# Feed-forward stage: the last round's four up tiles in a row, and the down products before them taken between the last gate's operations

## The chip, the cores and the metric

The kernel runs on one core of one Trainium2 chip. The metric is the device time of one execution in microseconds, lower is better. The core has TensorE (PE, matrix products), VectorE (DVE), ScalarE (ACT), GpSimd (POOL) and SyncE (SP, which only issues DMAs here). Each engine works through its own program in order and waits on semaphores for the others.

## The reference

One decoder layer is run for a prompt group (1024 tokens) and a sample group (8 times 4 tokens), 1056 tokens in all. The change lies in the last part of the layer, the feed-forward with a short convolution along the tokens:

```python
D_MODEL = 1024; D_FF = 2816; CONV_W = 3
def conv_ffn(h, conv_prev, w_up, conv_w, conv_b, w_down):
    T = h.shape[1]
    u = h @ w_up                                   # 1024 -> 2 * 2816
    up = jnp.concatenate([conv_prev.astype(u.dtype), u], axis=1)
    c = conv_b + sum(conv_w[j] * up[:, j:j + T] for j in range(CONV_W))
    gate, val = jnp.split(c, 2, axis=-1)
    return (jax.nn.silu(gate) * val) @ w_down, up[:, T:]

# in the layer: x = x + f, and after it y = rmsnorm(x, g_final)
```

## The kernel before

Everything is kept transposed: 128 features on the partitions, 1056 tokens along the free side, cut into three pieces of 352. Each fp32 product is made of three matmuls (high times high, high times low, low times high), in `products` (L276 to L281), which gives one semaphore step at its end. Such a product over a group of 128 features and 352 tokens is called a group here.

The stage `ffn_stage` takes the 2816 hidden features in 22 blocks, two blocks to a round, `ROUNDS` = 11, counted 0 to 10. A block has two up tiles, its gate half and its value half, so a round has four up tiles. An up tile is 3 groups of 24 matmuls. Numbered through, the last round has up tiles 40 to 43. The down products of a round are 24 groups of 6 matmuls, each added to `x` in SBUF.

**PE** (L2731 to L2761): `round_up(r, q, ..)` makes two up tiles (q = 0: gate and value of the first block, q = 1: of the second), `round_down(r, ..)` the 24 down groups of round r. A loop body holds two rounds; in each, the order is up (r, 0), down (r - 1), up (r, 1). After the loop only down (10) is left. The up groups use PSUM banks 0 to 3 in turn, the down groups banks 4 to 7, so PE can be four groups ahead of the engine that empties them.

**DVE**: `rows_of` scales an up tile out of PSUM into `ff_u` (L2869, L2871, L2873, one piece a group), `convolve` copies the state rows (L2882, L2883) and applies two taps (L2886, L2889), `multiply` makes the gated hidden block and splits it into high and low (L2899, L2902, L2904, L2907, L2909), `rest` makes the low part of a weight tile (L2857), `add_down` adds the 24 down groups of a round to `x` (L2918). `hidden_pair(r, ..)` is one round: the 24 adds of round r - 1 stand in one piece behind the rows of its second up tile, and before the second tile's convolution. In the last call `add_down(10, True)` the squares for the final norm are added too (L2926, L2928).

**ACT**: `rounded` makes the high part of a weight tile (L2768), `first_tap` brings the old state rows and applies the third tap with the bias (L2790, L2799), `gate` is the tanh (L2804), and after the last round it squares `x` (L2843).

**SP** brings weight tiles of 512 KB into two slots (`ff_slot`), a slot being free when `rest` has read it. High and low parts of up weights are in `ff_up` (two tiles), those of down weights in `ff_down` (two tiles, both blocks of a round). The last down weights, too, go to `ff_down`. `final_stage` follows: column sums, root, and the scaling of `x` with the output DMAs.

Of the kernel before, what the change touches and what calls it, by code (L numbers as in the profile page):

```python
# [18 lines left out]
ALU = mybir.AluOpType  # L19
# [8 lines left out]
C3 = T // 3  # L28
# [147 lines left out]
def third(ap, n):  # L176
    return ap[:, n * C3:(n + 1) * C3]
# [2493 lines left out]
def ffn_stage(k, H, L, hid, hid_full):  # L2671
# [6 lines left out]
    B = k.bank  # L2678
    UP, US = 2 + TP, 2 + TSEQ
    U = UP + NB * US  # L2680
    CV = U - 2
    ROUNDS = FK // 2
    S = {n: k.sem(f"ff_{n}") for n in (
        "past_in", "zero", "w_high", "w_low", "up_made", "up_taken", "past", "u_free", "c_first", "c_mid", "c_done", "cap", "tanh",
        "g_done", "hid_full", "hid_high", "hid_low", "down_made", "down_taken",
# [4 lines left out]
    with ExitStack() as ctx:  # L2690
# [10 lines left out]
        with nc.Block() as block:  # L2701
# [25 lines left out]
            @block.tensor  # L2727
            def _(pe):
                rows.pe(pe)

                def round_up(r, q, w_count):  # L2731

                    for j in range(2):
                        pe.wait_ge(S["w_low"], w_count + j)
                        t = 4 * r + 2 * q + j
                        for n in range(3):
                            pe.wait_ge(S["up_taken"], 3 * t + n + 1)
                            products(pe, B[(3 * (2 * q + j) + n) % 4][:, 0:C3], lambda a, kk: up[:, j, a, kk * P:(kk + 1) * P],
                                     lambda b, kk: third((H, L)[b][:, kk, :], n), DK, S["up_made"])

                def round_down(r, buf, w_count):
# [12 lines left out]
                round_up(0, 1, 3)  # L2754
                with pe.Fori(0, (ROUNDS - 1) // 2) as i:
                    for a in range(2):
                        r = 2 * i + a + 1
                        round_up(r, 0, 6 * r - 1)
                        round_down(r - 1, a, 6 * r + 2)
                        round_up(r, 1, 6 * r + 3)  # L2760
                round_down(ROUNDS - 1, (ROUNDS - 1) % 2, 6 * ROUNDS)  # L2761

            @block.scalar
            def _(act):
                def rounded(dst, j, count):
# [9 lines left out]
                def down_tile(r, e, j):  # L2775

                    act.wait_ge(S["down_taken"], DG * (r - 1) + 4)
                    rounded(down[:, j], e % 2, 3 * r + e // 2)
                rounded(up[:, 0], 0, 1)
                rounded(up[:, 1], 1, 1)  # L2780
                rows.act(act)
# [24 lines left out]
                def round_pair(r, more_up):  # L2806
# [16 lines left out]
                    first_tap(2 * r + 1, 0)  # L2823
                    if more_up:
                        up_tile(r + 1, 1, 1)
                    first_tap(2 * r + 1, 1)
                    gate(2 * r + 1)
                    if more_up:
                        down_tile(r + 1, 2, 0)
                        down_tile(r + 1, 3, 1)  # L2830
                    else:
                        down_tile(ROUNDS, 0, 0)
                        down_tile(ROUNDS, 1, 1)
                round_pair(0, True)
                with act.Fori(1, ROUNDS - 1) as r:
                    round_pair(r, True)
# [9 lines left out]
            def _(dve):  # L2846
# [45 lines left out]
                    dve.wait_ge(S["cap"], t + 2)  # L2892
                    dve.sem_inc(S["u_free"], 1)

                def multiply(i, q, buf):
# [8 lines left out]
                    dve.scalar_tensor_tensor(full[:, TP:T].rearrange("p (b n) -> p b n", b=NB), seg(th_[:, :], 0), 0.5,  # L2904
                                             seg(cv_[:, 1, :], 0), ALU.mult, ALU.mult).then_inc(S["hid_full"], 1)
                    dve.wait_ge(S["hid_full"], 2 * (i + 2))
                    dve.tensor_copy(high, full).then_inc(S["hid_high"], 1)  # L2907
                    dve.wait_ge(S["hid_high"], i + 1)
                    dve.tensor_tensor(low, full, high.bitcast(F32), ALU.subtract).then_inc(S["hid_low"], 1)  # L2909

                def add_down(r, last=False):

                    for m in range(DK):
                        for n in range(3):
                            g = 3 * m + n
                            dve.wait_ge(S["down_made"], DG * r + g + 1)
                            xs = third(k.x[:, m, :], n)
                            dve.tensor_tensor(xs, xs, B[4 + g % 4][:, 0:C3], ALU.add).then_inc(S["down_taken"], 1)  # L2918
                        if last and m >= 1:
                            add_squares(m - 1)  # L2920

# [8 lines left out]
                def hidden_pair(r, buf, add, more_up):  # L2930
                    n_tile = 6 * r - 2
                    rows_of(2 * r, 0, 0)
                    convolve(2 * r, 0)
# [8 lines left out]
                    if more_up:  # L2942
                        rest(up[:, 0], 0, n_tile + 6)
                    convolve(2 * r + 1, 0)
                    rows_of(2 * r + 1, 1, 1)
                    if more_up:
                        rest(up[:, 1], 1, n_tile + 7)
                    convolve(2 * r + 1, 1)
                    for j in range(2):
                        rest(down[:, j], j, n_tile + (8 if more_up else 6) + j)  # L2950
                    multiply(2 * r + 1, 1, buf)
                hidden_pair(0, 0, False, True)
                with dve.Fori(0, (ROUNDS - 3) // 2) as i:
                    for a in range(2):
                        hidden_pair(2 * i + a + 1, (a + 1) % 2, True, True)
                hidden_pair(ROUNDS - 2, (ROUNDS - 2) % 2, True, True)
                hidden_pair(ROUNDS - 1, (ROUNDS - 1) % 2, True, False)
                add_down(ROUNDS - 1, True)
                add_squares(DK - 1)


# [184 lines left out]
```

## Time and profile before

| | us |
|---|---|
| median of 3 runs | 2385.03 |
| lowest and highest run | 2373.6, 2385.66 |
| the profiled execution's own time | 2375.47 |
| its span, first to last instruction | 2373.8 |
| PE busy | 2198.0 |
| DVE busy | 1334.7 |
| ACT busy | 667.5 |

PE is the busiest engine and its matmuls overlap each other, so its busy time is no measure of peak. The feed-forward is the last stretch, from about 1556 us on. What an edit is worth is read from the waits of PE there, and from what each of the other engines had still to do when PE waited. Times below are from the start of the span.

### The profile page before, as it was taken

The numbers are of one execution on the slowest core, as the hardware profiler recorded it, in microseconds if no ns is written. First come the engines' busy times: TensorE is split into PE (matmuls) and PEld (weight loads), VectorE is DVE, ScalarE is ACT, GpSimd is POOL, SyncE is SP. The second block draws the span as 40 slices with busy tenths as digits, with TensorE's granted clock in tenths as the row PEclk, the third lists the DMA queues.
The fourth block names the chain that finished last, engine by engine and source line by source line (L and its number), as shares of the span: only waits on it lengthen the run. The fifth ranks groups of instructions, "written<-read, shape, count | busy, mean of one in ns | idle before, by whom it ended". The sixth has DMA issues, their size and how long they took to land. (4 is left out here: it accounts for less than half of the span.)

```text
span 2373.8 us, 51243 instructions
## 1 busy us (share of the span) xinstructions
PE 2198.0 (93%) x20986; PEld 2035.5 (86%) x20986; DVE 1334.7 (56%) x2616; ACT 667.5 (28%) x1348; POOL 118.5 (5%) x194
## 2 busy tenths in 40 slices
PE   7999999987879799988999997989999999999995
PEld 6999777766668799985899987989999999999995
DVE  6357555553355455543762264456666666666656
ACT  5110344443342444431131142221221111222111
POOL 0000100005300111110000000000000000000000
PEclk9999999998979999997999998999999999999997
DMA  4111100007523000013002252021111111111102
GB/s 154 45 45 45 39 12 12 6 1 193 139 92 101 25 4 4 4 24 122 28 20 97 80 189 78 19 69 45 45 55 45 48 34 45 46 54 54 45 21 78
DMA packets 81831, 134.07 MB, mean 56 GB/s; under 512 B 27185, under 2 KB 57778, under 8 KB 81490
## 3 DMA queue, kind: packets, MB, share of 16 engines
q1 hardware_dynamic: 70482, 119.22, 15.5%
q0 software_dynamic: 4224, 8.13, 1.3%
q10 hardware_dynamic: 6912, 3.54, 0.6%
q8 instruction: 174, 2.85, 0.5%
q14 instruction: 39, 0.32, 0.0%
HBM read 121.58 MB, written 9.29 MB: 55 GB/s over the span
## 5 line engine op out<-in xcount | busy, mean ns | idle before, releaser
L280 PE MATMUL psum<-high,ff_up 128*128 128x352 f32 x2112 | 517.3, 326 | 6.1 <-DVE ff_u L2873 3.8
L280 PEld LDWEIGHTS psum<-high,ff_up 128*128 128x128 f32 x2112 | 370.5, 189 | 8.1 <-DVE ff_u L2873 5.0
L280 PE MATMUL psum<-low,ff_up 128*128 128x352 f32 x1056 | 341.1, 323 | 0.0
L280 PE MATMUL psum<-hid,ff_down 128*128 128x352 f32 x1584 | 259.5, 325 | 12.1 <-issue 12.1
L280 PEld LDWEIGHTS psum<-hid,ff_down 128*128 128x128 f32 x1584 | 257.9, 189 | 12.4 <-issue 12.4
L446 PE MATMUL psum<-h_high,pj_part 128*128 128x352 f32 x960 | 242.5, 331 | 14.7 <-DVE h_low L553 14.6
L2918 DVE TENSOR_TENSOR x<-x,psum 128x352 f32<-128x352 f32 x264 | 137.1, 521 | 114.8 <-PE psum L280 114.8
L280 PEld LDWEIGHTS psum<-low,ff_up 128*128 128x128 f32 x1056 | 199.3, 189 | 0.0
L446 PEld LDWEIGHTS psum<-h_high,pj_part 128*128 128x128 f32 x960 | 172.0, 191 | 20.3 <-issue 10.4
L446 PE MATMUL psum<-h_low,pj_part 128*128 128x352 f32 x480 | 157.4, 328 | 0.0
L2768 ACT ACTIVATE ff_up<-ff_slot 128x1024 fp32r<-128x1024 f32 x44 | 46.2, 1051 | 391.1 <-PE psum L280 384.7
L2799 ACT ACTIVATE ff_c<-ff_u,vecs 128x1072 f32<-128x1072 f32 x44 | 56.5, 1285 | 180.8 <-DVE ff_u L2873 142.8
L280 PE MATMUL psum<-m_high,mo_part 128*128 128x352 f32 x384 | 94.9, 329 | 8.7 <-DVE mo_part L350 8.7
L822 PEld LDWEIGHTS psum<-mp_v,mp_pT 128*128 128x128 f32 x576 | 72.5, 195 | 29.4 <-ACT mp_pT L892 22.9
L280 PE MATMUL psum<-m_high,mq_part 128*128 128x352 f32 x384 | 94.6, 328 | 3.2 <-DVE mq_part L350 3.2
L446 PEld LDWEIGHTS psum<-h_low,pj_part 128*128 128x128 f32 x480 | 91.8, 191 | 1.0
L1847 PE MATMUL psum<-rc_W 64*64 64x64 f32 x1296 | 89.6, 223 | 1.4 <-ACT rc_MV L1895 0.3
L822 PE MATMUL psum<-mp_v,mp_pT 128*128 128x64 f32 x576 | 76.2, 279 | 12.7 <-ACT mp_pT L892 12.7
L280 PEld LDWEIGHTS psum<-m_high,mo_part 128*128 128x128 f32 x384 | 68.4, 193 | 8.9 <-DVE mo_part L350 8.9
L802 PE MATMUL psum<-mp_kT,mp_qT 96*128 96x512 f32 (+2 forms) x192 | 74.3, 497 | 0.0
L1853 PE MATMUL psum<-rc_W 64*64 64x64 f32 x1024 | 73.2, 218 | 0.0
L1847 PEld LDWEIGHTS psum<-rc_W 64*64 64x64 f32 x1296 | 65.7, 134 | 6.2 <-ACT rc_W L1893 2.6
(427 smaller groups left out, 4280.1 us busy)
## 6 DMA issues: line engine op xcount, KB each, us to landing
ff_slot<-in_w_up SPq DMA_DIRECT2D x44, 512.0 KB, 3.6
ff_slot<-in_w_down SPq DMA_DIRECT2D x22, 512.0 KB, 3.6
pj_slot<-in_w_in SPq DMA_DIRECT2D x20, 512.0 KB, 3.6
mk_slot<-in_w_mkv SPq DMA_DIRECT2D x16, 512.0 KB, 3.8
mz_k<-in_memk SPq DMA_DIRECT2D x8, 1024.0 KB, 5.6
mz_v<-in_memv SPq DMA_DIRECT2D x8, 1024.0 KB, 8.2
ms_keys<-in_lat SPq DMA_DIRECT2D x56, 128.0 KB, 2.8
ms_keys<-in_lat POOLq DMA_DIRECT2D x48, 128.0 KB, 3.0
```

What stands on the lines that cost most here:

```text
L280: mm = pe.matmul(ps, w(a, kk), rhs(b, kk), start=(kk == 0 and n == 0), stop=(kk == nk - 1 and n == 2))
L446: mm = pe.matmul(ps, part[:, j, a, kk * P:(kk + 1) * P], third((H, L)[b][:, kk, :], n), start=(kk == 0 and i == 0), stop=(kk == DK - 1 and ...
L802: mm = pe.matmul(B[2 * (i % 2) + c // 512][:, 0:w], qT[0:QH, j, i * P:(i + 1) * P], kT[h % 3][0:QH, c:c + w], start=True, stop=True)
L822: mm = pe.matmul(B[6][:, 0:HD], pT[:, i % 2, t * P:(t + 1) * P], v[:, t, h * HD:(h + 1) * HD], start=(t == 0), stop=(t == i))
L1847: mm = pe.matmul(PV[hf][h, at(64 * q)], W[h, p, N_, :], W[h, p, TT_, :], start=True, stop=True)
L1853: mm = pe.matmul(PY[hf][h, at(128 * q + 64)], W[h, p, NT_, :], W[h, p, N_, :], start=True, stop=True)
L2768: act.activation(dst[:, 0], slot[:, j], ACT.Copy).then_inc(S["w_high"], 1)
L2799: act.activation(cv[:, j, :], u[:, j, 2:U], ACT.Identity, bias=k.vecs[:, bass.ds(b0, 1)], scale=k.vecs[:, bass.ds(w2, 1)]).then_inc(S["c_f ...
L2918: dve.tensor_tensor(xs, xs, B[4 + g % 4][:, 0:C3], ALU.add).then_inc(S["down_taken"], 1)
```

## The change

In round 10 PE makes all four up tiles in a row, then down (9), then down (10). For that, round 9 is written out behind the loop (`middle(LAST - 1, ..)`), and the loop runs over four pairs of rounds, not five. On DVE the last round has its own function, `last_pair`: the 24 adds of round 9 are given out through `between` among the last tile's convolution, the weights' low parts and the five operations of the last `multiply`. The last down weights can't go to `ff_down`, which down (9) still reads, and go to `ff_up` instead, each when the up tile that held that place is done (`last_down`).

```diff
@@ PE
-                with pe.Fori(0, (ROUNDS - 1) // 2) as i:
+                def middle(r, a):
+                    round_up(r, 0, 6 * r - 1)
+                    round_down(r - 1, a, 6 * r + 2)
+                    round_up(r, 1, 6 * r + 3)
+                with pe.Fori(0, (ROUNDS - 3) // 2) as i:
                     for a in range(2):
-                        r = 2 * i + a + 1
-                        round_up(r, 0, 6 * r - 1)
-                        round_down(r - 1, a, 6 * r + 2)
-                        round_up(r, 1, 6 * r + 3)
-                round_down(ROUNDS - 1, (ROUNDS - 1) % 2, 6 * ROUNDS)
+                        middle(2 * i + a + 1, a)
+                middle(LAST - 1, LAST % 2)
+                round_up(LAST, 0, 6 * LAST - 1)
+                round_up(LAST, 1, 6 * LAST + 3)
+                round_down(LAST - 1, (LAST - 1) % 2, 6 * LAST + 2)
+                round_down(LAST, LAST % 2, 6 * ROUNDS, up)
@@ ACT
+                def last_down(j):
+                    act.wait_ge(S["up_made"], 3 * (4 * LAST + 2 + j + 1))
+                    rounded(up[:, j], j, 3 * ROUNDS)
                     first_tap(2 * r + 1, 0)
                     if more_up:
                         up_tile(r + 1, 1, 1)
+                    else:
+                        last_down(0)
                     first_tap(2 * r + 1, 1)
                     gate(2 * r + 1)
                     if more_up:
                         down_tile(r + 1, 2, 0)
                         down_tile(r + 1, 3, 1)
                     else:
-                        down_tile(ROUNDS, 0, 0)
-                        down_tile(ROUNDS, 1, 1)
+                        last_down(1)
@@ DVE, in multiply: between(2) behind the first product and behind
@@ the second, between(1) behind the copy to high
+                def last_pair(r, buf):
+                    n_tile, added = 6 * r - 2, [0]
+                    def between(n):
+                        for g in range(added[0], added[0] + n):
+                            add_group(r - 1, g)
+                        added[0] += n
+                    rows_of(2 * r, 0, 0)
+                    convolve(2 * r, 0)
+                    rest(up[:, 0], 0, n_tile + 4)
+                    rows_of(2 * r, 0, 1)
+                    rest(up[:, 1], 1, n_tile + 5)
+                    convolve(2 * r, 1)
+                    multiply(2 * r, 0, buf)
+                    rows_of(2 * r + 1, 1, 0)
+                    convolve(2 * r + 1, 0)
+                    rest(up[:, 0], 0, n_tile + 6)
+                    rows_of(2 * r + 1, 1, 1)
+                    between(1)
+                    convolve(2 * r + 1, 1)
+                    between(3)
+                    rest(up[:, 1], 1, n_tile + 7)
+                    between(2)
+                    multiply(2 * r + 1, 1, buf, between)
+                    between(DG - added[0])
```

The first place is the end of PE's program. Here `ff_up` and `ff_down` are the weight tiles, `high` and `low` the stage's input, `hid` the gated hidden blocks. Before, from the loop's end on:

```order
L280 MATMUL psum<-high,ff_up 128x352 x2
L280 MATMUL psum<-low,ff_up 128x352
L280 MATMUL psum<-high,ff_up 128x352
L2755 REGISTER_ALU
L2755 COMPARE_AND_BRANCH
L280 MATMUL psum<-hid,ff_down 128x352 x144
L2701 UNCONDITIONAL_BRANCH
```

The changed kernel, at the end of PE's program:

```order
L280 MATMUL psum<-high,ff_up 128x352 x2
L280 MATMUL psum<-low,ff_up 128x352
L280 MATMUL psum<-high,ff_up 128x352
L280 MATMUL psum<-hid,ff_down 128x352 x144
L280 MATMUL psum<-hid,ff_up 128x352 x144
L2702 UNCONDITIONAL_BRANCH
```

Behind the last up tile now stand two runs of 144 matmuls, those of round 9 with `ff_down` and those of round 10 with weights in `ff_up`, where one stood, and the branch of the loop is further ahead, behind round 8.

The second place is DVE around the last two up tiles. Before, from the rows of the last up tile to the first adds of round 10 (the 24 adds of round 9 stood much earlier, as one row of x24):

```order
L2873 TENSOR_TENSOR ff_u<-psum,acc 128x8x4
L2882 COPY ff_cap<-ff_u 128x2
L2883 COPY ff_cap<-ff_u 128x16
L2886 SCALAR_TENSOR_TENSOR ff_c<-ff_u,vecs,ff_c 128x1072
L2889 SCALAR_TENSOR_TENSOR ff_c<-ff_u,vecs,ff_c 128x1072
L2857 TENSOR_TENSOR ff_down<-ff_slot,ff_down 128x1024 x2
L2899 SCALAR_TENSOR_TENSOR ff_t<-ff_t,ff_c 128x1072
L2902 SCALAR_TENSOR_TENSOR hid_full<-ff_t,ff_c 128x1024
L2904 SCALAR_TENSOR_TENSOR hid_full<-ff_t,ff_c 128x32
L2907 CAST hid<-hid_full 128x1056
L2909 TENSOR_TENSOR hid<-hid_full,hid 128x1056
L2918 TENSOR_TENSOR x<-x,psum 128x352 x6
```

The changed kernel, from the second tap of that last up tile on (L2901; L2930 are the adds, L2869 is a weight tile's low part):

```order
L2901 SCALAR_TENSOR_TENSOR ff_c<-ff_u,vecs,ff_c 128x1072
L2930 TENSOR_TENSOR x<-x,psum 128x352 x3
L2869 TENSOR_TENSOR ff_up<-ff_slot,ff_up 128x1024
L2930 TENSOR_TENSOR x<-x,psum 128x352 x2
L2911 SCALAR_TENSOR_TENSOR ff_t<-ff_t,ff_c 128x1072
L2930 TENSOR_TENSOR x<-x,psum 128x352 x2
L2915 SCALAR_TENSOR_TENSOR hid_full<-ff_t,ff_c 128x1024
L2917 SCALAR_TENSOR_TENSOR hid_full<-ff_t,ff_c 128x32
L2930 TENSOR_TENSOR x<-x,psum 128x352 x2
L2921 CAST hid<-hid_full 128x1056
L2930 TENSOR_TENSOR x<-x,psum 128x352
L2924 TENSOR_TENSOR hid<-hid_full,hid 128x1056
```

One add stands before this piece, behind the rows of the last up tile, and the rest follow behind its end: the adds of round 9 that stood in one run before the last gate's work are spread over it.

## Rows read from the trace of the kernel before

**Rows 1.** The page: span and part 1, busy us with share and count.

```profile
span 2373.8 us, 51243 instructions
PE 2198.0 (93%) x20986; PEld 2035.5 (86%) x20986; DVE 1334.7 (56%) x2616; ACT 667.5 (28%) x1348; POOL 118.5 (5%) x194
```

**Rows 2.** Waits of PE, 1560 to 2374: waiter, cause, total us, times, longest.

```profile
PE psum L280 <- issue: 12.1, 1, 12.1
PE psum L280 <- DVE ff_u L2873: 3.8, 4, 1.1
```

**Rows 3.** Timeline of PE, 2310 to 2330 and 2346 on: start, us, work [idle before].

```profile
2310.67 0.32 PE L280 MATMUL psum<-high,ff_up 128*128 128x352 f32 x1
2323.09 7.10 PE L280 MATMUL psum<-hid,ff_down 128*128 128x352 f32 x31 [12.10 <-issue]
...
2346.18 2.26 PE L280 MATMUL psum<-hid,ff_down 128*128 128x352 f32 x13
```

**Rows 4.** Timeline of DVE, last up tile's end to the last hidden block.

```profile
2311.03 0.49 DVE L2871 TENSOR_TENSOR ff_u<-psum,acc 128x320 f32<-128x320 f32 x1 [3.36 <-PE psum L280]
...
2316.05 2.36 DVE L2857 TENSOR_TENSOR ff_down<-ff_slot,ff_down 128x1024 fp32r<-128x1024 f32 x2 [0.18 <-DVE ff_c L2889]
...
2321.73 1.26 DVE L2909 TENSOR_TENSOR hid<-hid_full,hid 128x1056 fp32r<-128x1056 f32 x1
```

**Rows 5.** Stretches: bounds, length, busy of PE, PEld, DVE, ACT, POOL, granted clock, DMA.

```profile
2313.00:2323.00 10.00, 0.00 (x0) 0.00 (x0) 9.66 (x11) 2.87 (x3) 0.00 (x0) 0.53 0.10 41
2323.00:2327.00 4.00, 3.91 (x13) 3.94 (x14) 0.53 (x2) 0.00 (x0) 0.00 (x0) 0.50 0.00 0
2327.00:2331.00 4.00, 4.00 (x25) 4.00 (x25) 2.08 (x4) 1.09 (x1) 0.00 (x0) 0.98 0.00 0
```

**Rows 6.** Timeline of DVE: first and last of 24 adds of round 9.

```profile
2265.42 0.52 DVE L2918 TENSOR_TENSOR x<-x,psum 128x352 f32<-128x352 f32 x1 [0.39 <-PE psum L280]
...
2287.70 0.52 DVE L2918 TENSOR_TENSOR x<-x,psum 128x352 f32<-128x352 f32 x1 [0.44 <-PE psum L280]
```

**Rows 7.** Timeline of DVE: up tile 41's last piece; behind the adds; up tile 42's last piece.

```profile
2264.45 0.49 DVE L2871 TENSOR_TENSOR ff_u<-psum,acc 128x320 f32<-128x320 f32 x1 [2.06 <-PE psum L280]
...
2288.14 1.22 DVE L2857 TENSOR_TENSOR ff_up<-ff_slot,ff_up 128x1024 fp32r<-128x1024 f32 x1
2289.27 0.16 DVE L2882 COPY ff_cap<-ff_u 128x2 f32<-128x2 f32 x1
...
2292.30 1.27 DVE L2899 SCALAR_TENSOR_TENSOR ff_t<-ff_t,ff_c 128x1072 f32<-128x1072 f32 x1 [0.18 <-DVE ff_c L2889]
...
2296.89 0.95 DVE L2869 TENSOR_TENSOR ff_u<-psum,acc 128x352 f32<-128x352 f32 x2
2299.37 0.49 DVE L2871 TENSOR_TENSOR ff_u<-psum,acc 128x320 f32<-128x320 f32 x1 [1.52 <-PE psum L280]
```

**Rows 8.** Timeline of ACT, the last round.

```profile
2266.31 1.04 ACT L2768 ACTIVATE ff_up<-ff_slot 128x1024 fp32r<-128x1024 f32 x1
...
2300.04 1.28 ACT L2799 ACTIVATE ff_c<-ff_u,vecs 128x1072 f32<-128x1072 f32 x1 [32.58 <-DVE ff_u L2873]
```

**Rows 9.** The page, part 6: DMA issues, KB each, median us to landing.

```profile
ff_slot<-in_w_down SPq DMA_DIRECT2D x22, 512.0 KB, 3.6
```

**Rows 10.** Timeline of PE: start of the loop's last pass, 2160 to 2180.

```profile
2170.88 0.42 PE L280 MATMUL psum<-high,ff_up 128*128 128x352 f32 x1 [0.88 <-DVE ff_u L2873]
```

**Rows 11.** Stretch of the loop's first pass, columns as in group 5.

```profile
1607.00:1747.00 140.00, 139.74 (x864) 139.45 (x862) 92.58 (x145) 27.50 (x33) 0.00 (x0) 1.00 0.15 46
```

**Rows 12.** Timeline of DVE: adds of round 10, and the last.

```profile
2335.55 0.94 DVE L2918 TENSOR_TENSOR x<-x,psum 128x352 f32<-128x352 f32 x2
2336.85 0.52 DVE L2918 TENSOR_TENSOR x<-x,psum 128x352 f32<-128x352 f32 x1 [0.35 <-PE psum L280]
2337.29 1.25 DVE L2926 TENSOR_TENSOR acc<-acc,ff_c 128x1056 f32<-128x1056 f32 x1
...
2348.48 0.52 DVE L2918 TENSOR_TENSOR x<-x,psum 128x352 f32<-128x352 f32 x1 [0.36 <-PE psum L280]
```

More of the change, by code:

```diff
@@ L2682, in ffn_stage @@
     ROUNDS = FK // 2
+    LAST = ROUNDS - 1
     S = {n: k.sem(f"ff_{n}") for n in (
@@ L2739, in round_up, with round_down @@
                                      lambda b, kk: third((H, L)[b][:, kk, :], n), DK, S["up_made"])
-                def round_down(r, buf, w_count):
+                def round_down(r, buf, w_count, down=down):
                     pe.wait_ge(S["w_low"], w_count)
@@ L2893, in convolve, with multiply @@
                     dve.sem_inc(S["u_free"], 1)
-                def multiply(i, q, buf):
+                def multiply(i, q, buf, between=lambda n: None):
                     dve.wait_ge(S["tanh"], i + 1)
                     dve.scalar_tensor_tensor(th[:, :], th[:, :], 1.0, cv[:, 0, :], ALU.add, ALU.mult).then_inc(S["g_done"], 1)
+                    between(2)
                     dve.wait_ge(S["g_done"], i + 1)
@@ L2905, in multiply, with add_group @@
                                              seg(cv_[:, 1, :], 0), ALU.mult, ALU.mult).then_inc(S["hid_full"], 1)
+                    between(2)
                     dve.wait_ge(S["hid_full"], 2 * (i + 2))
                     dve.tensor_copy(high, full).then_inc(S["hid_high"], 1)
+                    between(1)
                     dve.wait_ge(S["hid_high"], i + 1)
                     dve.tensor_tensor(low, full, high.bitcast(F32), ALU.subtract).then_inc(S["hid_low"], 1)
+                def add_group(r, g):
+                    dve.wait_ge(S["down_made"], DG * r + g + 1)
+                    xs = third(k.x[:, g // 3, :], g % 3)
+                    dve.tensor_tensor(xs, xs, B[4 + g % 4][:, 0:C3], ALU.add).then_inc(S["down_taken"], 1)
                 def add_down(r, last=False):
@@ L2914, in add_down @@
                         for n in range(3):
[L2915 to L2918, printed above, removed]
+                            add_group(r, 3 * m + n)
                         if last and m >= 1:
@@ L2928, in add_squares, with hidden_pair @@
                         dve.tensor_copy(k.acc, cv_[:, 0, 0:T]).then_inc(S["added"], 1)
-                def hidden_pair(r, buf, add, more_up):
+                def last_pair(r, buf):
[15 more added lines that the diff above has]
+                    rows_of(2 * r + 1, 1, 1)
+                    between(1)
+                    convolve(2 * r + 1, 1)
+                    between(3)
+                    rest(up[:, 1], 1, n_tile + 7)
+                    between(2)
+                    multiply(2 * r + 1, 1, buf, between)
+                    between(DG - added[0])
+                def hidden_pair(r, buf, add):
                     n_tile = 6 * r - 2
@@ L2941, in hidden_pair @@
                     rows_of(2 * r + 1, 1, 0)
-                    if more_up:
-                        rest(up[:, 0], 0, n_tile + 6)
+                    rest(up[:, 0], 0, n_tile + 6)
                     convolve(2 * r + 1, 0)
                     rows_of(2 * r + 1, 1, 1)
-                    if more_up:
-                        rest(up[:, 1], 1, n_tile + 7)
+                    rest(up[:, 1], 1, n_tile + 7)
                     convolve(2 * r + 1, 1)
                     for j in range(2):
-                        rest(down[:, j], j, n_tile + (8 if more_up else 6) + j)
+                        rest(down[:, j], j, n_tile + 8 + j)
                     multiply(2 * r + 1, 1, buf)
-                hidden_pair(0, 0, False, True)
+                hidden_pair(0, 0, False)
                 with dve.Fori(0, (ROUNDS - 3) // 2) as i:
                     for a in range(2):
[L2955 to L2958, printed above, removed]
+                        hidden_pair(2 * i + a + 1, (a + 1) % 2, True)
+                hidden_pair(LAST - 1, (LAST - 1) % 2, True)
+                last_pair(LAST, LAST % 2)
+                add_down(LAST, True)
                 add_squares(DK - 1)
```

## The prediction

> **What bounds the kernel now.** I read the page's busy shares first, then the list of PE's waits in the feed-forward, then the timelines of PE, DVE and ACT over the last two rounds. PE is busy 2198.0 of 2373.8 us [rows 1], and in the feed-forward it waits only twice in a way that counts [rows 2]: once for 12.1 us, and four times for 3.8 us in all. The long wait lies between the last up tile, which ends at 2310.67 + 0.32 = 2310.99, and the first down matmul of round 10 at 2323.09 [rows 3]. It is labelled "issue", but DVE's timeline names the cause: the low part of the last hidden block ends at 2321.73 + 1.26 = 2322.99 [rows 4], and down (10) needs it. DVE itself works nearly without a pause there, 9.66 of 10 us from 2313 to 2323 [rows 5]. So the end of the stage is a chain: last up tile, its rows, its convolution, the weights' low parts, the gate, then 24 down groups. Round 9's down products, which depend on none of that, were done earlier.
>
> The wait has a second price. PE's clock, at full speed up to the last up tile, is granted at 0.53 on average between 2313 and 2323, with no matmul, and still at 0.50 for the first 4 us of work, that is at 1.2 of 2.4 GHz [rows 5]. The price: PE needs from 2323.09 to 2346.18 + 2.26 = 2348.44, which is 25.35 us, for the 24 groups [rows 3]. The same 24 groups of round 9 came at a pace of (2287.70 - 2265.42) / 23 = 0.969 us, 23.25 us for 24 [rows 6]. So 2.10 us are lost to the slow start.
>
> **The change part by part.**
>
> PE's order: the same 432 matmuls in round 10, moved. Up tiles 42 and 43 follow up tile 41, which ends at 2264.4 in the old trace (its last piece is picked up at 2264.45 [rows 7]). One up tile takes 2311.03 - 2299.37 = 11.66 us [rows 4, 7]. So tile 42 ends at 2276.1 and tile 43 at 2287.7, and down (9) begins at 2287.7, where it needs only what was ready long before. If DVE keeps pace it ends at 2287.7 + 23.25 = 2311.0, just where the last up tile ended before.
>
> What must be ready for tile 43: its weights. ACT makes the high part from 2266.31 to 2267.35 [rows 8]; in the old order DVE's low part stood behind the 24 adds, at 2288.14 [rows 7], now it follows at once, 2267.4 to 2268.6. It is needed at 2276.1, 7.5 us of cover. Tile 42's weights were ready before the adds in both orders. The two DMAs for the last down weights keep their place on SP's queue, and the second can be issued some 20 us earlier, since `rest` frees the slot earlier; landing takes 3.6 us [rows 9], and they are wanted from 2278 and 2290 on.
>
> DVE, step by step. Durations are start to start in [rows 7]: a convolution 2292.30 - 2289.27 = 3.0 (2.85 and a pause), a `multiply` 2296.89 - 2292.30 = 4.6, a weight tile 1.2, rows that are all there 1.4 to 1.5, an add 0.47 when two stand together [rows 12], and ACT's first tap 1.28 [rows 8]. From 2268.6: convolution of tile 41 to 2271.6, `multiply` to 2276.2, rows of tile 42 to 2277.6, ACT's tap to 2278.9, convolution to 2281.9, down weights (first) to 2283.1, two pieces of tile 43 to 2284.4, then a wait for PE, third piece to 2288.4. The first down group is made at 2288.7, its add ends at 2289.3, while ACT works on the tap till 2289.7, so that add is free. Convolution of tile 43 to 2292.5; adds 1 to 3 to 2293.9; weights (second) to 2295.1; adds 4, 5 to 2296.1; then the `multiply` with its five adds in between to 2302.9; then 13 adds against groups already waiting or coming.
>
> PE against this: group g needs the add of group g - 4. Group 5 could start at 2292.6 and gets its bank at 2293.0 to 2293.1, 0.5 lost. Groups 6 to 11 find banks. Group 12 waits some 0.1 to 0.2 for add 8 (behind the second product of `multiply`), group 15 some 0.3 to 0.4 for add 11 (behind the last operation). That makes about 1.0 us of stalls. It can't be below 0. For the other end I let each of the three places be 1 us later than I have it, 4 us in all. I take 1.0, the worked-out value, because every duration in it is a row. Down (9) then ends at 2312.0. The hidden block is ready at 2302.9 and the weights at 2295.1, so down (10) follows at once, 9 us of cover.
>
> Down (10): 24 groups at 0.969, now with the clock up from the start, 23.25 us, ending at 2335.3. DVE has 3 adds and one square sum in each 2.91 us there and still waited 0.35 [rows 12], so it keeps pace as it did. The o_conv DMA comes some 20 us earlier and nothing waits for it but the end.
>
> The loop: PE loses 0.88 us at the start of the loop's last pass [rows 10], and 3.8 us over the four jumps back [rows 2], though no up tile started inside a pass waits. The changed kernel jumps back three times; round 9 follows the loop by falling through. Does that cost the same? The trace of before can't show it, since that exit lay under the 12.1 us wait. Ends: nothing saved, or 1.05. The nearest row is the entry into the loop's body, 864 matmuls with 139.74 of 140 us busy [rows 11], so coming to new code in order costs nothing that shows. I take 0.9 saved.
>
> Here a page gives another price. The Trainium skill, Advanced Engine Details and Errata, section Control Flow Timing, puts a compare-and-branch at about 108 ns. By that the saving would be 0.1 and the sum 13.3; the trace has 0.88 to 1.05 for the whole jump, so the measured row decides.
>
> Behind the last add (2348.48 [rows 12]) nothing changes: final sums, root, scaling, output. It moves forward as a block, 25 us long in both.
>
> Sum against the profiled execution: -12.10 (wait) - 2.10 (slow clock) + 1.0 (stalls) - 0.9 (jump) = -14.1 us. Its time was 2375.47, so a like execution would take 2361.4. But the median of the runs shown is 2385.03, 9.6 above it, with one run at 2373.6 and two near 2385. The stretch that I change is short and nothing in it explains that spread, so I carry the difference over: 2385.03 - 14.1 = 2370.9. Between 10.1 (4 us stalls, no jump saved) and 15.3 (no stalls, 1.05) are the ends of the sum.
>
> **The rivals.**
>
> DVE becomes the bound in down (9). It has 0.7 + 3.0 + 1.2 + 4.6 = 9.5 us of work other than adds and 24 times 0.47 = 11.3 of adds in 23.25 us, 2.5 us to spare. If nothing of the 9.5 overlapped with PE's banks, the stalls would be 9.5 and the time 2385.03 - 14.1 + 8.5 = 2379.4; half of it gives 2375. For it: the adds in the old trace are 0.52 us each with a pause before them [rows 6]. Against: four banks carry 3.9 us of PE, and no stretch between adds is longer than 3.3.
>
> The change doesn't do what it says: the wait comes back between down (9) and down (10), because weights or the hidden block are late. That needs them over 9 us later than worked out, and gives about 2385. Against it stands that each step is a row.
>
> Slower: written-out code can't be fed to PE. Behind the loop now stand 432 + 576 = 1008 matmuls instead of 144, each run once. If PE lost the 0.95 us of a jump back at every up group's length, 24 matmuls, over the 864 more, that would be 36 pauses, 34 us, and 2405. It decides from 14.1 / 864 = 16 ns a matmul on. Against: the first pass of the loop is new code as well, 864 matmuls, without a pause [rows 11].
>
> **How the numbers follow.** My forecast, a gain of 10 to 15 us with 14.1 likeliest: 0.82. DVE as bound, 2374 to 2379: 0.10. The wait comes back, 2385: 0.04. Code that can't be fed, 2405: 0.04. The predicted time is 2371. The range goes down to 2373.6 - 15.3 = 2358 for a median at the low end of the spread, and up to 2377, which takes in 2385.66 - 10.1 = 2375.6 and most of the second case. A difference of 0.5%, about what a measurement of this kernel can tell from no change, is 11.9 us, so faster means below 2373.1. The forecast lies 2 us inside it, and I give it 0.88 of the first case: 0.72, with 0.01 of the second. Within 0.5%: 0.10 + 0.09 + 0.04 = 0.23. Slower: 0.04.
>
> **What would show it.** Right: no PE wait over 1 us between up tile 40 and the end of down (10); granted clock 1.00 all through; the low part of the last hidden block ends some 9 us before down (9) does; down (10) in 23.3 us; three jumps with about 0.9 each, none in front of round 9; small PE waits for adds at groups 5, 12 and 15. Wrong: a new wait for DVE's adds of several us in down (9), a wait between the last two runs of 144 matmuls, or pauses within the written-out round 9. If the profile shows all of it right and the median still moved by under 12 us, the spread of the runs did that, not a step of the sum.

## The result and the profile after

The changed kernel takes 2364.55 us (median of 7 runs, 2358.85 to 2365.92). Seven runs of the kernel before beside it have a median of 2382.96 (2373.6 to 2386.1). The ratio is 0.9935, 95% interval 0.9918 to 0.9953, a gain of about 15.5 us (11 to 20); the two medians by themselves are 18.4 us apart. The profiled execution took 2365.02 us, with a span of 2363.4.

The page of the changed kernel, to be read beside [rows 1]: the work is the same, the span is 10.4 us shorter.

```profile
span 2363.4 us, 51169 instructions
PE 2198.6 (93%) x20986; PEld 2035.6 (86%) x20986; DVE 1333.3 (56%) x2616; ACT 666.9 (28%) x1348; POOL 118.2 (5%) x194
```

The waits of PE in the feed-forward, which answer to [rows 2] (waiter, cause, total us, times, longest). The wait of 12.1 us is gone, three pauses at jumps are left where there were four, and a wait of 0.8 us for an add (L2930) is new. The waits of the final norm's L221 and L230 stand in both kernels.

```profile
PE psum L221 <- PEq L2702: 3.4, 1, 3.4
PE psum L280 <- DVE ff_u L2885: 3.0, 3, 1.2
PE psum L280 <- DVE x L2930: 0.8, 1, 0.8
PE psum L230 <- DVE nfin_col L245: 0.6, 1, 0.6
```

DVE's timeline in the changed kernel, from the last piece of the last up tile on (start, us, work, idle before). It answers to [rows 4].

```profile
2290.69 0.49 DVE L2883 TENSOR_TENSOR ff_u<-psum,acc 128x320 f32<-128x320 f32 x1 [3.36 <-PE psum L280]
...
2291.66 0.52 DVE L2930 TENSOR_TENSOR x<-x,psum 128x352 f32<-128x352 f32 x1 [0.39 <-PE psum L280]
2292.68 0.17 DVE L2894 COPY ff_cap<-ff_u 128x2 f32<-128x2 f32 x1 [0.50 <-ACT ff_c L2810]
...
2295.71 1.39 DVE L2930 TENSOR_TENSOR x<-x,psum 128x352 f32<-128x352 f32 x3 [0.18 <-DVE ff_c L2901]
...
2304.21 1.25 DVE L2924 TENSOR_TENSOR hid<-hid_full,hid 128x1056 fp32r<-128x1056 f32 x1
2305.38 2.39 DVE L2930 TENSOR_TENSOR x<-x,psum 128x352 f32<-128x352 f32 x5
2308.21 0.52 DVE L2930 TENSOR_TENSOR x<-x,psum 128x352 f32<-128x352 f32 x1 [0.44 <-PE psum L280]
```

The first add comes at once and costs nothing, since ACT's tap is not done until 2292.65. Adds 1 to 3 wait behind the convolution till 2295.71, and there PE has its one wait. The low part of the last hidden block ends at 2304.21 + 1.25 = 2305.46, some 9 us before down (10) wants it. From 2308 on DVE waits for PE again before each add, as in [rows 6]. PE's side of it, and the end:

```profile
2290.49 5.01 PE L280 MATMUL psum<-hid,ff_down 128*128 128x352 f32 x30
2296.29 18.66 PE L280 MATMUL psum<-hid,ff_down 128*128 128x352 f32 x114 [0.79 <-DVE x L2930]
2314.79 23.42 PE L280 MATMUL psum<-hid,ff_up 128*128 128x352 f32 x144
...
2341.62 3.44 PE L221 MATMUL psum<-masks,acc 128*88 128x1 f32 x24 [3.42 <-PEq L2702]
```

The stretches (bounds, length, busy of PE, PEld, DVE, ACT, POOL, granted clock, DMA) from round 7 to the last up tile, and of all 288 down matmuls. The first contains the place behind the loop where round 9 is written out: no pause. The clock stays at 1.00, against 0.50 in [rows 5].

```profile
2035.00:2290.00 255.00, 255.00 (x1577) 255.00 (x1576) 170.23 (x262) 53.15 (x63) 0.00 (x0) 1.00 0.15 48
2290.70:2338.20 47.50, 46.72 (x288) 46.13 (x286) 37.54 (x65) 10.86 (x10) 0.00 (x0) 1.00 0.03 9
```

### A measure that is finer than the whole time

The feed-forward starts, by its first up product, at 1558.46 us in the first trace of the kernel before, and at 1562.42 in that of the changed one, though the code ahead of it is the same. In twelve traces it starts between 1554.15 and 1565.92. So I count each trace from its first up product to the end of its span. The two traces of each of three kernels differ by 0.1 to 0.4 us in that (`no_loop_2` is `no_loop` once more).

| kernel | first up product | span | from there to the end |
|---|---|---|---|
| before | 1558.46 | 2373.8 | 815.3 |
| before, second trace (`before_again`) | 1556.03 | 2371.6 | 815.6 |
| `written_out` | 1562.44 | 2377.1 | 814.7 |
| `filler` | 1561.23 | 2373.0 | 811.8 |
| `adds_first` | 1565.16 | 2376.8 | 811.6 |
| `adds_last` | 1554.15 | 2363.2 | 809.1 |
| changed | 1562.42 | 2363.4 | 801.0 |
| changed, second trace (`after_again`) | 1556.81 | 2357.7 | 800.9 |
| `between_taps` | 1565.92 | 2366.0 | 800.1 |
| `no_loop` | 1554.53 | 2350.9 | 796.4 |
| `no_loop_2` | 1562.79 | 2359.6 | 796.8 |
| `tail_filler` | 1560.36 | 2355.1 | 794.7 |

Within the stretch the pauses, too, need care. The list counts idle time from the modelled end of a matmul. Where nothing is waited for, a matmul starts every 0.162 us but is shown with 0.32 us, so a delay under 0.16 us leaves no idle time, and a longer one shows with 0.16 us too little. An example is a jump in `between_taps`:

```profile
1753.88 0.32 PE L280 MATMUL psum<-high,ff_up 128*128 128x352 f32 x1
1754.88 0.42 PE L280 MATMUL psum<-high,ff_up 128*128 128x352 f32 x1 [0.68 <-DVE ff_u L2885]
1755.14 0.32 PE L280 MATMUL psum<-low,ff_up 128*128 128x352 f32 x1
```

Two steps take 1755.14 - 1753.88 = 1.26 us, where 0.32 would do: the jump costs 0.94, and the list says 0.68. Of the missing 0.26 us, 0.16 are the modelled end and 0.10 the slower step behind the pause. The difference is 0.26 us at all 30 jumps of the nine traces with a loop. What is called "from start to start" below is counted in this way.

### The profile page after: what moved, and what is told of

It reads as the page before. It is cut to its first block and busy times, and to the rows that moved or that the text cites. A ratio compares the mean times of both kernels' runs of the same rounds, so it can differ in the third digit from the quotient of the medians.

```text
span 2363.4 us, 51169 instructions
## 1 busy us (share of the span) xinstructions
PE 2198.6 (93%) x20986; PEld 2035.6 (86%) x20986; DVE 1333.3 (56%) x2616; ACT 666.9 (28%) x1348; POOL 118.2 (5%) x194
## 5 line engine op out<-in xcount | busy, mean ns | idle before, releaser
L446 PE MATMUL psum<-h_high,pj_part 128*128 128x352 f32 x960 | 242.8, 331 | 14.9 <-DVE h_low L553 14.8
L280 PE MATMUL psum<-hid,ff_down 128*128 128x352 f32 x1440 | 234.4, 324 | 0.8 <-DVE x L2930 0.8
L280 PEld LDWEIGHTS psum<-hid,ff_down 128*128 128x128 f32 x1440 | 232.8, 188 | 1.1 <-DVE x L2930 1.1
L2930 DVE TENSOR_TENSOR x<-x,psum 128x352 f32<-128x352 f32 x264 | 136.3, 520 | 105.6 <-PE psum L280 105.3
```

Of the source, the lines that this page charges most:

```text
L280: mm = pe.matmul(ps, w(a, kk), rhs(b, kk), start=(kk == 0 and n == 0), stop=(kk == nk - 1 and n == 2))
L446: mm = pe.matmul(ps, part[:, j, a, kk * P:(kk + 1) * P], third((H, L)[b][:, kk, :], n), start=(kk == 0 and i == 0), stop=(kk == DK - 1 and ...
```

## The experiments

### Both kernels again

No edit. The changed kernel:

> The changed kernel once more, to hold the next three against on the same chip. My theory puts its whole gain in the last round: 12.10 us of wait, 2.10 us of slow clock, 0.9 us of one jump back, less the waits for banks (0.79 in the first trace of it), so 14.3 us from the start of the loop's second pass to the end, and 14 to 15 us in the whole. The rival, that part of the gain lies before the feed-forward or is spread of the runs, expects a gain in the whole that differs from the stretch's by more than 3 us.

Measured: 2364.53 us, median of 8, ratio to the kernel before 0.995 (0.9934 to 0.9966). The stretch is 14.4 to 14.7 us shorter in the pairs of traces, which lies inside both intervals of the whole (11 to 20 and 8 to 16 us) and within 3 us of their centres (15.5 and 11.9). Nothing speaks for the rival, but the intervals are too wide to shut it out by themselves. The kernel before:

> The kernel before once more, for a second trace of it. Its runs lie at 2374 to 2376 and at 2383 to 2386. If the spread lies in the feed-forward, my taking it over unchanged was unfounded; I expect the stretch from the loop's second pass to the end to be 626.0 us as in the first trace, within 0.3, and the difference to lie before 1556 us.

Measured: ratio to itself 1.0003 (0.9986 to 1.0019). From PE's restart at the second pass (1745.51, where [rows 2] has the first of its four pauses) to the end it is 2371.6 - 1745.51 = 626.1, as in the first trace (2373.8 - 1747.80 = 626.0). The spread lies ahead of the feed-forward, as the starts in the table show. The two traces here are both from executions at the low end, so one at 2383 to 2386 was not seen. In the twelve traces most of the difference has arisen in the first 802 us: of the same PE instructions, those that `adds_last`, the earliest, starts there come 11.4 us later in `adds_first` and 8.5 us later in `between_taps`, and at the first up product the two are 11.0 and 11.8 us behind. What makes it there stays open.

### The loop's jump

The kernel before, with rounds 9 and 10 behind the loop, in the old order:

```diff
-                with pe.Fori(0, (ROUNDS - 1) // 2) as i:
+
+                def middle(r, a):
+                    round_up(r, 0, 6 * r - 1)
+                    round_down(r - 1, a, 6 * r + 2)
+                    round_up(r, 1, 6 * r + 3)
+                with pe.Fori(0, (ROUNDS - 3) // 2) as i:
                     for a in range(2):
-                        r = 2 * i + a + 1
-                        round_up(r, 0, 6 * r - 1)
-                        round_down(r - 1, a, 6 * r + 2)
-                        round_up(r, 1, 6 * r + 3)
+                        middle(2 * i + a + 1, a)
+                middle(ROUNDS - 2, 0)
+                middle(ROUNDS - 1, 1)
```

> The kernel before with round 9 of PE written out behind the loop (the loop over four pairs of rounds, not five), in the old order. Theory: one jump back less and falling through costs nothing: PE has three waits of about 1 us in the loop instead of four and none in front of round 9, 0.9 us faster from the loop's second pass on. Rival: leaving the loop costs what a jump costs, and the time is the same.

Measured: PE's waits list has three pauses and no fourth.

```profile
PE psum L280 <- issue: 12.1, 1, 12.1
PE psum L221 <- PEq L2701: 3.4, 1, 3.4
PE psum L280 <- DVE ff_u L2877: 2.9, 3, 1.2
```

The stretch is 814.7, 0.7 to 0.9 us below the two traces of the kernel before. The whole doesn't tell it (0.9999, 0.9986 to 1.0011). Leaving the loop costs nothing that shows. From start to start the three jumps cost 3.72 us, and the four of the kernel before 4.85 and 4.86, so one jump less saves 1.1 us here. Part of it is lost again, since the 144 matmuls behind the long wait took longer than in either trace of the kernel before (25.35 [rows 3] and the first row here; the second is `written_out`):

```profile
2320.74 25.50 PE L280 MATMUL psum<-hid,ff_down 128*128 128x352 f32 x144 [12.10 <-issue]
2325.93 25.81 PE L280 MATMUL psum<-hid,ff_down 128*128 128x352 f32 x144 [12.10 <-issue]
```

### The wait and the clock

The kernel before, with work of no use in the wait:

```diff
+                pe.wait_ge(S["down_taken"], DG * (ROUNDS - 1) + 4)
+                for _ in range(70):
+                    pe.matmul(B[7][:, 0:C3], up[:, 1, 0, 0:P], third(H[:, 0, :], 0), start=True, stop=True)
                 round_down(ROUNDS - 1, (ROUNDS - 1) % 2, 6 * ROUNDS)
```

> The kernel before with 70 matmuls of no use (128x352, into down bank 7, which group 3 of round 10 overwrites) in PE's wait in front of round 10's down products; nothing else is changed. It parts the wait from the clock. Theory: the hidden block is ready when it was, so the down products start when they did, but the granted clock stays at 1.00 and the 24 groups take 23.3 us instead of 25.35: 2.1 us faster than the kernel before. Rival: the slow start has another cause (the first adds, banks, weights), the 24 groups still take about 25 us and the time is unchanged.

Measured: ratio 0.9977 (0.9961 to 0.9993), stretch 811.8, 3.6 to 3.8 us less than before. PE's timeline (L2763 is the filler) and its stretches:

```profile
2313.35 11.37 PE L2763 MATMUL psum<-high,ff_up 128*128 128x352 f32 x70
2325.62 9.62 PE L280 MATMUL psum<-hid,ff_down 128*128 128x352 f32 x58 [0.90 <-issue]
```

```profile
2325.60:2349.10 23.50, 23.48 (x144) 23.23 (x144) 17.45 (x29) 7.64 (x7) 0.00 (x0) 1.00 0.00 1
2352.50:2354.80 2.30, 2.19 (x24) 2.13 (x24) 0.00 (x0) 1.32 (x2) 0.00 (x0) 0.87 0.05 11
```

The down products start as late as before (the hidden block ends at 2324.26 + 1.26 = 2325.52), and the 144 matmuls take 23.5 us at a clock of 1.00 where the kernel before takes 25.35 at 0.50 and then 1.00 [rows 3, 5]. So the clock alone was worth 1.85 us against the first trace, and 2.0 and 2.3 against the 25.50 and 25.81 us of the two other traces in the old order. The 2.10 that I had lies inside that. Some 0.2 us more of the gain come from shorter pauses at the four jumps (4.61 us against 4.85). The other 1.5 us I hadn't expected: the 24 column sums of the final norm (L221), the same instructions, take 2.19 us here and 3.65 in the kernel before, whose row is:

```profile
2351.80:2355.50 3.70, 3.65 (x24) 3.59 (x24) 0.00 (x0) 1.28 (x1) 0.00 (x0) 0.50 0.01 2
```

### The place of the adds

The changed kernel's PE order, with the 24 adds in one piece ahead of the last convolution:

```diff
                     rows_of(2 * r + 1, 1, 1)
-                    between(1)
+                    between(DG)
                     convolve(2 * r + 1, 1)
-                    between(3)
                     rest(up[:, 1], 1, n_tile + 7)
-                    between(2)
-                    multiply(2 * r + 1, 1, buf, between)
-                    between(DG - added[0])
+                    multiply(2 * r + 1, 1, buf)
```

> The changed kernel with all 24 adds of round 9 in one piece behind the rows of the last up tile, ahead of its convolution, where they stood in every other round. It keeps PE's new order and takes away the interleaving. Theory: the adds last until PE ends down (9), and the convolution, the weights' low part and the gate come behind: 2.85 + 1.2 + 4.6 = 8.7 us, so PE waits about 9 us in front of down (10) and has a slow clock for about 2 us of loss again: 10 us slower than the changed kernel, 4 us faster than the kernel before. Rival: the order of PE alone brings the gain and the time is that of the changed kernel.

Measured: ratio 0.9972 (0.9962 to 0.9983), stretch 811.6, 10.7 us longer than the changed kernel. PE and DVE, and the clock:

```profile
2293.17 23.42 PE L280 MATMUL psum<-hid,ff_down 128*128 128x352 f32 x144
2324.64 1.26 DVE L2924 TENSOR_TENSOR hid<-hid_full,hid 128x1056 fp32r<-128x1056 f32 x1
2326.00 8.20 PE L280 MATMUL psum<-hid,ff_up 128*128 128x352 f32 x37 [9.41 <-issue]
```

```profile
2316.60:2326.00 9.40, 0.00 (x0) 0.03 (x1) 8.96 (x11) 0.00 (x0) 0.00 (x0) 0.69 0.11 43
2326.00:2331.00 5.00, 5.00 (x19) 5.00 (x20) 1.04 (x2) 0.00 (x0) 0.00 (x0) 0.56 0.01 3
```

The old wait is back with 9.41 of its 12.10 us. Down (9) runs without a stall, 23.42 us for its 144 matmuls. PE's order alone gives 3.7 to 3.9 us of the gain. The other extreme, all adds behind the last gated block:

```diff
                     rows_of(2 * r + 1, 1, 1)
-                    between(1)
                     convolve(2 * r + 1, 1)
-                    between(3)
                     rest(up[:, 1], 1, n_tile + 7)
-                    between(2)
-                    multiply(2 * r + 1, 1, buf, between)
-                    between(DG - added[0])
+                    multiply(2 * r + 1, 1, buf)
+                    between(DG)
```

> The changed kernel with all 24 adds of round 9 behind the last gated block. Theory: PE fills its four banks and then waits for the first add, from 3.9 us after the last up tile to about 11 us after it: a wait of 7 us inside down (9), whose groups then come at PE's pace, none in front of down (10); 6.5 us slower than the changed kernel, and up to 2 us more if the clock falls in that wait; 6 to 8 us faster than the kernel before. Rival: with four banks between them the order of the adds doesn't matter, and the time is that of the changed kernel.

Measured: ratio 0.9984 (0.9968 to 1.0), stretch 809.1, 8.1 to 8.2 us longer than the changed kernel. PE makes its four groups, waits 7.48 us for the first free bank, and restarts at a clock of 0.52:

```profile
2281.91 4.04 PE L280 MATMUL psum<-hid,ff_down 128*128 128x352 f32 x24
2292.86 1.81 DVE L2930 TENSOR_TENSOR x<-x,psum 128x352 f32<-128x352 f32 x4
2293.43 22.02 PE L280 MATMUL psum<-hid,ff_down 128*128 128x352 f32 x120 [7.48 <-DVE x L2930]
```

```profile
2286.00:2293.40 7.40, 0.00 (x0) 0.00 (x0) 7.12 (x9) 0.01 (x1) 0.00 (x0) 0.67 0.04 15
2293.40:2299.00 5.60, 5.57 (x20) 5.57 (x21) 2.31 (x5) 0.00 (x0) 0.00 (x0) 0.52 0.00 0
```

7.48 less the 0.79 of the changed kernel is 6.7. The 120 matmuls behind the wait take 22.02 us, where 119 steps of 0.162 and a last one of 0.32 make 19.6: 2.4 us more for the slow restart. That is 9.1 us, of which 1.0 came back by chance in this trace, 0.3 in shorter pauses at the jumps and 0.7 in the column sums at the end (2.79 us against 3.44). Of the whole gain, then, more than half hangs on the adds being spread.

### The last wait in the down products

The changed kernel, with one add moved between the last convolution's two taps:

```diff
-                def convolve(i, j):
+                def convolve(i, j, between=lambda n: None):
@@ its two taps
                     dve.scalar_tensor_tensor(cv[:, j, :], u[:, j, 1:U - 1], tap(1), cv[:, j, :], ALU.mult, ALU.add)\
                        .then_inc(S["c_mid"], 1)
+                    between(1)
@@ last_pair
-                    convolve(2 * r + 1, 1)
-                    between(3)
+                    convolve(2 * r + 1, 1, between)
+                    between(2)
```

> The changed kernel with one of the adds of round 9 moved between the two taps of the last convolution (it was behind both). Theory: the only PE wait of the changed kernel inside the down products, 0.79 us in front of group 5, ends, because the add of group 1 is done some 1 us before it is wanted; no new one comes, so 0.8 us faster than the changed kernel, to be seen in the trace rather than in the time. Rival: the wait moves on to group 6 or 12 and the time is the same.

Measured: stretch 800.1, 0.8 to 0.9 us below the changed kernel. The ratio of 0.994 (0.9918 to 0.9962) can't tell the two apart. DVE's add of group 1 starts right behind the first tap, and PE's waits list holds no add any more:

```profile
2295.82 1.33 DVE L2898 SCALAR_TENSOR_TENSOR ff_c<-ff_u,vecs,ff_c 128x1072 f32<-128x1072 f32 x1
2297.06 0.52 DVE L2931 TENSOR_TENSOR x<-x,psum 128x352 f32<-128x352 f32 x1
...
2308.24 2.36 DVE L2931 TENSOR_TENSOR x<-x,psum 128x352 f32<-128x352 f32 x5
```

```profile
PE psum L280 <- DVE ff_u L2885: 2.5, 3, 1.1
PE psum L230 <- DVE nfin_col L245: 0.6, 1, 0.6
```

That looks like the theory, number and all, and it isn't. The timeline of PE has down (9) and down (10):

```profile
2293.47 24.30 PE L280 MATMUL psum<-hid,ff_down 128*128 128x352 f32 x144
2317.61 23.42 PE L280 MATMUL psum<-hid,ff_up 128*128 128x352 f32 x144
```

Down (9) still takes 24.30 us, 0.88 more than the 23.42 it takes in `adds_first` without a stall; in the changed kernel it is 2296.29 + 18.66 - 2290.49 = 24.46. So the move gained 0.16 us, and the rival was right: the wait moved on. From start to start groups 6, 8, 10, 12 and 15 each fall back a little, by 0.4, 0.1, 0.1, 0.2 and 0.2 us, which is too little for the list to name. The last of them shows why: group 15 needs add 11, which stands behind the whole gate and ends at about 2308.24 + 0.5 = 2308.7, while group 15 was due at 2293.47 + 15 * 0.97 = 2308.0. PE has to fall behind by about that much in any case, and the wait at group 5 had only taken it all at once. The rest of the 0.8 to 0.9 us is chance: the three jumps cost 3.28 us here against 3.82 and 3.58 in the changed kernel's two traces, and what follows the last down product is 25.0 us long against 25.2 and 25.4.

### All of PE's code in line

On top of that:

```diff
-                with pe.Fori(0, (ROUNDS - 3) // 2) as i:
+                for i in range((ROUNDS - 3) // 2):
                     for a in range(2):
                         middle(2 * i + a + 1, a)
```

> The one with the add between the taps, and PE's loop over rounds 1 to 8 written out as well, so that PE has 4752 matmuls of the stage in line and jumps nowhere. Theory: what PE loses at a jump back is the jump (1.20, 0.98 and 0.86 us in the changed kernel), written-out code costs nothing, and the three waits go: 3.0 us faster than with the loop, 3.8 faster than the changed kernel. Rival, the slower case of my prediction: long code can't be fed and shows pauses, with 0.95 us for every 24 matmuls some 130 us slower, with a few pauses a few us slower.

Measured: 2355.6 us, ratio 0.9918 (0.9897 to 0.9939), stretch 796.4. Once more, on another occasion:

> The kernel with PE's loop written out once more, beside the next one and the kernel before. In its trace the stretch from the first up product to the end was 14.6 us shorter... of which 14.4 for the order and 4.5 for bank wait and jumps, 19 us in all against the kernel before. The ratio of the runs should be 0.992 within its interval, as in its first runs; the rival, that its first 0.9918 was luck of the spread, expects the ratio of the changed kernel, 0.994 to 0.995.

Measured: 2360.08 us, ratio 0.9916 (0.9895 to 0.9937), stretch 796.8. The list has no wait of PE left from the first up product to the last down product. The lists of the kernels with a loop put the pauses at the jumps on DVE's `ff_u`. DVE's program is that of `between_taps` here and the pauses are gone, so the jumps made them:

```profile
PE psum L221 <- PEq L2702: 3.4, 1, 3.4
PE psum L230 <- DVE nfin_col L245: 0.6, 1, 0.6
```

The interval of the second comparison ends just below the 0.994 of its rival. From the first up product to the last down product it takes 771.8 us in both traces (in `no_loop_2` 2324.74 + 9.84 - 1562.79), `between_taps` 775.1: 3.3 us less, of which 2.5 are the pauses that its waits list names and 0.8 the 0.26 us that the list leaves out at each of the three. The small delays in down (9) are still there (24.33 us in `no_loop_2`). Long code in line costs nothing: the slower rival of the prediction is out over 4752 matmuls. That the kernel in line is faster than the changed one rests on the traces (4.1 to 4.6 us); the intervals of the ratios overlap.

### The column sums at the end

On top of that, to test what the filler had shown by the way:

```diff
                 round_down(LAST, LAST % 2, 6 * ROUNDS, up)
+                for _ in range(20):
+                    pe.matmul(B[0][:, 0:C3], up[:, 1, 0, 0:P], third(H[:, 0, :], 0), start=True, stop=True)
```

> The same with 20 matmuls of no use (128x352, into up bank 0, which nothing reads any more) behind the last down products, in the 3.4 us in which PE waits for the final norm's column sums; nothing else is changed. It asks whether the length of these 24 small sums (3.65 us in the kernel before, 3.44, 2.87 and 2.19 in others, for the same instructions) hangs on the granted clock. Theory: with no pause ahead of them the clock stays at 1.00 and they take 2.2 us, each time, so the stretch from the last down product to the end is 23.9 us and not 24.6 to 25.4: 0.7 to 1.5 us faster. Rival: their length has another cause, or the fillers hold up the sums, and the stretch is as long or longer.

Measured: 2356.2 us, ratio 0.9912 (0.9896 to 0.9927), stretch 794.7. Its PE timeline (L2770 is the filler), then `no_loop_2` over the same instructions:

```profile
2331.98 3.37 PE L2770 MATMUL psum<-high,ff_up 128*128 128x352 f32 x20
2335.65 2.01 PE L221 MATMUL psum<-masks,acc 128*88 128x1 f32 x24 [0.30 <-PEq L2702]
2338.27 4.32 PE L230 MATMUL psum<-masks,nfin_col 88*128 88x88 f32 x24 [0.61 <-DVE nfin_col L245]
```

```profile
2338.00 3.31 PE L221 MATMUL psum<-masks,acc 128*88 128x1 f32 x24 [3.41 <-PEq L2702]
2341.92 5.42 PE L230 MATMUL psum<-masks,nfin_col 88*128 88x88 f32 x24 [0.61 <-DVE nfin_col L245]
```

The stretches of the sums have a granted clock of 1.00 here and 0.56 there:

```profile
2335.60:2337.70 2.10, 2.01 (x24) 1.95 (x24) 0.00 (x0) 1.29 (x2) 0.00 (x0) 1.00 0.01 4
```

```profile
2338.00:2341.40 3.40, 3.31 (x24) 3.22 (x24) 0.00 (x0) 1.30 (x2) 0.00 (x0) 0.56 0.01 2
```

From the last down product to the end of the span it is 2355.1 - 2332.14 = 23.0 us, against 24.6 and 25.0 in the two traces of the kernel without the filler and 25.4 in the kernel before. That is 1.6 to 2.1 us less, a little more than expected, because the next products (L230) run faster too. This is the fastest version here, 20.6 to 20.9 us below the kernel before in the stretch.

## Why the prediction was right, step by step

**The wait.** 12.10 us taken away whole: right. The new order on DVE came out to half a microsecond. I had the last hidden block 15.2 us behind the last up tile (2302.9 against 2287.7), the trace has 2305.46 against 2290.65, 14.8. With 9 us of cover nothing of it could reach PE. The two kernels with the adds elsewhere show that this is no matter of PE's order alone: they wait 9.41 and 7.48 us.

**The clock.** 2.10 us: right, and no sharper than the thing itself. The 144 matmuls take 23.42 us in the changed kernel and 25.35, 25.50 and 25.81 in the three traces in the old order, so it was worth 1.9 to 2.4 us by that, and 1.85 to 2.3 by the filler. I had set 25.35 against 24 times the pace of the adds, 23.25, and so left out that the last matmul also has to run out; that made 0.17 us.

**The stalls.** I had 1.0 us in three places, groups 5, 12 and 15. The changed kernel has 1.05 us from start to start, in one place, group 5. The size was right and the working only in part: I added up three waits as if they were independent. A group that comes late makes the next ones find their banks free, so what counts is the lateness that the slowest add forces, and `between_taps` shows that taking away one of the waits brings the others back. The rival in which DVE becomes the bound had a true core, four banks being all the cover there is, but needs a stretch without adds of the kind in `adds_last`.

**The jump.** 0.9 us for one jump less: right in kind, and a little small, since the row of 0.88 leaves out the 0.26 us that don't show as idle. From start to start the jumps cost 1.04 and 1.28 us less in the two pairs of traces, and 1.1 less in `written_out`, with three pauses left. That the pauses differ among themselves is part of these numbers. The Trainium skill's price for a compare-and-branch, about 108 ns (Advanced Engine Details and Errata, section Control Flow Timing), would have given 0.1; the traces have pauses of 0.66 to 1.20 us at the jumps back and none at the exit.

**The tail.** I said that it moves as a block, 25 us long in both. It was 25.4 and 25.2, and in other kernels 23.9 to 25.4 with the same instructions. This step was wrong in kind: its column sums run at whatever clock is granted at that moment. It cost little here by luck: in the first pair of traces it differed by 0.2 us, in the second not at all.

**The sum.** Of the first pair of traces, from start to start: 12.26 (wait, the 12.10 of the list and the 0.16 that it leaves out) + 1.93 (slow clock) + 1.04 (jumps) - 1.05 (stalls) + 0.21 (end) = 14.4 us, as the stretch has it; 14.1 was predicted. The prediction's lower end has a slip: 12.10 + 2.10 - 4 is 10.2, not 10.1.

**The time.** 2371.0 was predicted and 2364.55 measured, inside the range but 6.5 us off, and the gain of the runs of the first comparison is 15.5 us. The weak step was the base: I carried the difference between the profiled execution and the median of three runs over in full. With 19 and 31 runs the kernel before has medians of 2378.5 and 2377.2, so 2385.03 was a draw from the upper part of its spread; the changed kernel's profiled execution lay only 0.5 us above its median, not 9.6. "Nothing in the stretch explains the spread" was right; that the changed kernel's runs would lie in the same part of it was not supported by anything. That faster by over 0.5% was likely and not sure was fitting: the two comparisons give 0.65% and 0.5%.

## What to carry to other kernels

When an engine's last work waits for a chain that starts with its own previous result, look for work of the same engine that doesn't depend on the chain and was done earlier only because the loop's body had that order; holding one such piece back fills the wait. It pays in full only if the engine that empties its results is told to do so among the chain's operations: here 24 adds in one piece before or behind the chain gave back 8 to 11 of 14 us, while adds spread over the chain gave back 1.0. Count stalls from start to start as well as by the list of idle times: here a wait left the list, and the time, by chance, fell by just its length, while the stall had only been cut into pieces too small to be named. And size such a change in a stretch of the trace that starts behind the spread of the rest, since medians of the kernel before ranged from 2376.9 to 2385.0 us, more than half of the gain.

## What the runs showed of the hardware

The same 24 matmuls of one column took 2.01 us with a granted clock of 1.00 and 3.65 us with 0.50, with 2.19, 2.79, 2.87, 3.27, 3.31 and 3.44 in other kernels. In all but the one with fillers ahead of them PE had stood idle for 3.4 us before. How much of them ran slow differed from kernel to kernel, so a later edit can gain or lose 1.5 us at the end of this program without touching it.

A jump back in PE's loop of two rounds (864 matmuls) left pauses of 0.66 to 1.20 us by the list, and cost 0.92 to 1.46 us from start to start; within one trace of the kernel before the pauses ranged from 0.66 to 1.14. Entering the loop, leaving it and running 4752 matmuls in line left none.

A matmul of 128x352 started every 0.162 us at a granted clock of 1.00. The first step behind a pause, still at 1.00, took 0.26 us, at all 30 jumps.
